# Moving one of twelve float16 residual subtractions of each expert item from VectorE to GpSimd

## What is computed

```python
logits = (h @ w_router + b_router).astype(jnp.float32)
top_val, top_idx = lax.top_k(logits, 4)          # 4 of 32 experts a token
gate = jax.nn.softmax(top_val, axis=-1)
...
gu = xblk @ w_gate_up[e] + b_gate_up[e]
g_lin = jnp.minimum(gu[:, :1024], 7.0)
u_lin = jnp.clip(gu[:, 1024:], -7.0, 7.0)
act = g_lin * jax.nn.sigmoid(1.702 * g_lin) * (u_lin + 1.0)
return act @ w_down[e] + b_down[e]
...
y = y.at[row_tok].add(yb * row_g[:, None])       # rows added back into the stream
```

## Time and profile before

| what | value |
|---|---|
| three timed runs | 2106.95, 2105.22, 2104.69 us; median 2105.22 us |
| the profiled execution's own time | 2105.01 us, its span 2103.2 us |
| TensorE matmul busy | 1981.9 us (94%) |
| VectorE busy | 1527.3 us (73%) |
| ScalarE busy | 1425.2 us (68%) |
| GpSimd busy | 531.3 us (25%) |
| HBM traffic | 234 GB/s over the span; 320 to 340 GB/s in the expert stage |

### The profile page before, as it was taken

How to read it: one execution, slowest core, us unless ns; L and a number is a source line. 1 busy time by engine, 2 the same in 40 slices (tenths; PEclk the granted TensorE clock), 3 DMA queues, 4 the chain that set the end, 5 groups by cost and what they waited for, 6 DMA issues and landing times.

```text
span 2103.2 us, 60172 instructions
## 1 busy us (share of the span) xinstructions
PE 1981.9 (94%) x24649; PEld 1664.8 (79%) x24649; DVE 1527.3 (73%) x2026; ACT 1425.2 (68%) x1810; POOL 531.3 (25%) x413
## 2 busy tenths in 40 slices
PE   6999999999979769999999999999999999999997
PEld 3444874443554469999999999999999999999997
DVE  5331334554472278888998999899899989989995
ACT  4330423666563458777888888788888878888884
POOL 2222211323551232112222321222132122223111
PEclk8999999999999879999999999999999999999999
DMA  5111100000143468999999999999999999999996
GB/s 170 40 41 60 41 21 1 1 1 0 31 138 119 147 208 305 312 330 309 331 323 339 337 324 323 340 328 323 339 335 337 324 334 333 326 337 326 341 321 214
DMA packets 142367, 479.14 MB, mean 228 GB/s; under 512 B 15135, under 2 KB 30239, under 8 KB 142240
## 3 DMA queue, kind: packets, MB, share of 16 engines
q1 hardware_dynamic: 129440, 444.13, 58.8%
q0 software_dynamic: 12864, 34.11, 6.8%
HBM read 457.34 MB, written 34.87 MB: 234 GB/s over the span
## 4 chain that ended last, share of the span: by engine, by line
PE 30%; DVE 15%; issue 12%; ACT 4%; DMA 3%; DVEq 1%; POOL 0%; POOLq 0%; SPq 0%; ACTq 0%
PE banks L1721 28%; DVE region_c L1020 9%; DVE region_b L1557 2%; DMA region_a<-w_down_dram 2%; DVE region_b L1562 1%; ACT region_b L1404 1%; ACT region_b L1408 1%; PE banks L1687 1%; PE banks L1714 1%; ACT region_b L1394 1%; ACT region_b L1392 1%; DVE region_b L1578 1%; DVE region_b L1571 1%; DMA region_b<-rows_out,region_d 1%; DVE region_b L1567 0%
## 5 line engine op out<-in xcount | busy, mean ns | idle before, releaser
L1721 PE MATMUL banks<-region_b,region_c 128*128 128x144 f16 (+1 forms) x18432 | 1198.6, 227 | 32.1 <-DVE region_c L1020 25.3
L1721 PEld LDWEIGHTS banks<-region_b,region_c 128*128 128x128 f16 x18432 | 1181.3, 98 | 39.3 <-DVE region_c L1020 26.6
L1020 DVE TENSOR_TENSOR region_c<-region_a,region_c 128x2048 f16<-128x2048 f32 x256 | 574.4, 2286 | 4.8 <-DMA region_b<-rows_h,region_d 4.3
L1015 ACT ACTIVATE region_c<-region_a 128x2048 f16<-128x2048 f32 x256 | 475.5, 1904 | 22.9 <-PE banks L1721 17.4
L1335 POOL TENSOR_TENSOR region_d<-region_d 80x1 f32<-80x1 f32 x96 | 77.7, 810 | 961.4 <-DVE region_d L1530 643.5
L1020 DVE TENSOR_TENSOR region_c<-region_d,region_c 128x2048 f16<-128x2048 f32 x128 | 287.1, 2284 | 0.0
L1015 ACT ACTIVATE region_c<-region_d 128x2048 f16<-128x2048 f32 x128 | 237.9, 1918 | 0.0
L352 PE MATMUL banks<-region_a,region_d 128*128 128x512 f16 x960 | 209.7, 381 | 1.7 <-PEq L95 1.7
L1417 ACT ACTIVATE region_b<-banks,region_d 80x512 f32<-80x512 f32 x128 | 80.5, 678 | 163.9 <-PE banks L1714 163.9
L352 PEld LDWEIGHTS banks<-region_a,region_d 128*128 128x128 f16 x960 | 94.2, 98 | 117.4 <-issue 6.5
L1324 POOL DMA_INDIRECT region_b<-rows_h,region_d x64 | 136.0, 2125 | 38.0 <-issue 38.0
(11 more groups left out here) (287 smaller groups left out, 2165.7 us busy)
## 6 DMA issues: line engine op xcount, KB each, us to landing
region_d<-w_gate_up_dram SPq DMA_DIRECT2D x128, 1024.0 KB
region_a<-w_gate_up_dram SPq DMA_DIRECT2D x128, 1024.0 KB
region_a<-w_down_dram SPq DMA_DIRECT2D x128, 1024.0 KB
region_d<-w_in_dram SPq DMA_DIRECT2D x14, 1024.0 KB, 5.0
region_b<-x_dram SPq DMA_DIRECT2D x4, 1024.0 KB, 9.5
region_b<-w_out_dram SPq DMA_DIRECT2D x8, 512.0 KB, 3.6
rows_out<-region_b SPq DMA_DIRECT2D x8, 512.0 KB, 2.6
rows_h<-region_b SPq DMA_DIRECT2D x8, 512.0 KB, 2.6
```

The costliest lines, as they stand in the source:

```text
L1015: act.activation(part_hi[r][:, 2 * q:2 * q + 2, :], raw[r][:, 2 * q:2 * q + 2, :], ACT.Copy).then_inc(s_hi9, 1)
L1020: dve.tensor_tensor(part_lo[r][:, at, :], raw[r][:, at, :], part_hi[r][:, at, :], ALU.subtract).then_inc(s_lod, 1)
L1721: mm = pe.matmul(out_ap, a, b, start=(first and s == 0), stop=(k == KT - 1 and s == 2), skip_group_check=True)
```

## The change

The low part of the second half of chunk 4 (`POOL_HALF = (4, 1)`, the second half of the first down chunk) is subtracted by GpSimd, at the end of its item, behind the second scatter-add. VectorE skips it, so `s_lod` counts 11 halves an item and every wait on it is renumbered through `lows`. A new semaphore `s_plo` counts GpSimd's halves; SyncE waits for it before it loads into that half's slot, and TensorE waits for it at the start of down(0).

```diff
-        s_hi9, s_lod = sem("part_hi_ready"), sem("part_lo_ready")
+        s_hi9, s_lod, s_plo = sem("part_hi_ready"), sem("part_lo_ready"), sem("pool_part_lo_ready")
+        POOL_HALF = (4, 1)
+
+        def lows(i, m, q):
+            return i * 11 + (2 * m + q + 1 - ((m, q) >= POOL_HALF))
@@ sync, item_loads
                         for q in range(2):
-                            sp.wait_ge(s_lod, i * (2 * CH) + (2 * m + q + 1))
+                            if (m, q) == POOL_HALF:
+                                sp.wait_ge(s_plo, i + 1)
+                            else:
+                                sp.wait_ge(s_lod, lows(i, m, q))
                             load(sp, e if m < RING else e_next, (m + RING) % CH, q)
@@ gpsimd, item_rows
                     carry_wait(2, i * 3 + (1 if last else 2))
                     scatter(1)
+                    m, q = POOL_HALF
+                    r, at = m % RING, slice(2 * q, 2 * q + 2)
+                    pool.wait_ge(s_hi9, i * (2 * CH) + (2 * m + q + 1))
+                    pool.tensor_tensor(part_lo[r][:, at, :], raw[r][:, at, :], part_hi[r][:, at, :], ALU.subtract).then_inc(s_plo, 1)
@@ vector, low_part
                     for q in range(2):
-                        low_half(dve, c, j, q)
+                        if (j, q) != POOL_HALF:
+                            low_half(dve, c, j, q)
@@ tensor, gate, up and down
-                    pe.wait_ge(s_lod, i * (2 * CH) + (2 * half + 2))
+                    pe.wait_ge(s_lod, lows(i, half, 1))
...
-                    pe.wait_ge(s_lod, i * (2 * CH) + (2 * (2 + half) + 2))
+                    pe.wait_ge(s_lod, lows(i, 2 + half, 1))
...
-                    pe.wait_ge(s_lod, i * (2 * CH) + (2 * (4 + half) + 2))
+                    pe.wait_ge(s_lod, lows(i, 4 + half, 1))
+                    if half == 0:
+                        pe.wait_ge(s_plo, i + 1)
```

## The result

The changed kernel takes 2311.07 us in the median (2308.08 to 2314.2, 4 runs), the kernel before 2104.95 us beside it: 1.0982 times as long, with an interval of 1.0967 to 1.0998, or 206 us slower. The profiled execution took 2310.04 us with a span of 2308.1 us. In the new file line 1024 is VectorE's low part, 1371 GpSimd's, 1733 the expert matmuls, 1342 and 1336 the carry and the scatter-add, 1579, 1583 and 1590 the activation steps.

A forecast was written before the change was run, and what follows sets the result against it. TensorE, with almost no idle time to win, was taken as the bound, down(0) having to wait for GpSimd. 138 us of waits plus 58 us of clock on 2105.0 us gave 2301, said as 2300 us; range 2236 to 2345 us.

The forecast's parts named there:

- A: The forecast itself: down(0) waits for GpSimd and the clock falls in most of these waits; 2300 us, chance 0.77.
- The wait: Ahead of down(0), TensorE waits for GpSimd's half: about 5.4 us a narrow item, 3.85 us a wide one; 138 us net.
- The sum behind the second scatter-add: From the second scatter-add's end to down(0): 0.30 gap, 0.1 VectorE in flight, 4.07 subtraction, 0.1 signal, in us.
- The clock: TensorE's clock falls behind the new wait: 2.0 us a narrow item, about 1.2 us a wide one, 58 us together.
- The first gate half's 2.23 us: Extra time of the stage's first gate half, started at the lower clock: 9.03 us against 6.80 us for the next.
- the 1.8 us: Work lost at half speed after TensorE stood 5.62 us, the clock returning 3.65 us after its restart.
- The 0.88 us ahead of down(1): TensorE's idle stretch before down(1) in each of 26 narrow items goes away by itself, 23 us.
- VectorE beside GpSimd: VectorE loses about 4.07 us in its activation steps while GpSimd subtracts, hidden ahead of down(1) by 0.7 us.
- Loads: SyncE's load into that slot half is issued some 9 us later but still lands in time; costed at nothing.
- Rival B: Down(0) waits for GpSimd but the clock costs nothing or little: 2243 us, chance 0.12.
- Rival C: GpSimd gets its turn late behind busy VectorE, or VectorE's lost time sets down(1): 2372 us, chance 0.07.
- Rival D: At the start of down(0), GpSimd is done before TensorE comes, winning back at most 25.3 us: 2080 us, chance 0.02.

The follow-up runs named there:

- the filling matmuls: The changed kernel with 68 more matmuls of 128 columns, product unread, ahead of TensorE's wait for GpSimd's half: 2251.19 us, 1.0691 against the kernel before.
- the two-pass kernel: The kernel before, with down(1) in two passes, its first 48 matmuls waiting only for the first half of chunk 5: 2087.33 us, 0.9919.
- the one in VectorE's own idle time: The changed kernel with GpSimd given the second half of the next item's gate chunk 1 instead: 2105.83 us, 1.0014 against the kernel before.

## Why the prediction was right, and where its terms were off

The forecast was 2300 us, the median is 2311.07 us, in the range of 2236 to 2345 us, by the mechanism named as A.

- **The wait.** Forecast 138 us net of the 0.88 us stretches; the idle time ahead of the expert matmuls grew by 145.5 us and TensorE's as a whole by 140.3 us, since it idled 5.2 us less elsewhere. The waits themselves are 175.5 us in place of 160 to 170 us: 5.8 us a narrow item against 5.4, and 4.15 us a wide one against 3.85. The sum behind the second scatter-add came out at 4.5 us, as 0.30 + 0.1 + 4.07 + 0.1 had it, but that is luck between its terms: in the item shown GpSimd ended 4.09 us after the scatter-add, without the gap of 0.30 us, and TensorE started 0.44 us after GpSimd, not 0.1 us. GpSimd's own row reads 4.55 us instead of 4.07, because it starts inside the scatter-add's row.
- **The clock.** Forecast 2.0 us a narrow item, 1.2 us a wide one and 58 us in all; measured 8.61 - 6.16 = 2.45 us in the item shown, 57.2/26 = 2.2 us in the mean of the narrow items and 11.2/6 = 1.9 us in that of the wide ones, 64.6 us more busy time in all, and 60 us given back by the filling matmuls. The first gate half's 2.23 us was the nearer row, not the mean of it and the 1.8 us. Both terms were thus some way too small, and the sum with them: 196 us forecast, 205 us measured in the span. The upper bound has a slip as well: 2.8 us for each of 32 items is 90 us, not 87.
- **The 0.88 us ahead of down(1).** It went away in the changed kernel, as said. With the wait ahead of down(1) taken away by TensorE's order alone the kernel gained 16.6 us. Whether that is the most that a relief of VectorE could bring is not shown: in no run did the move to GpSimd relieve VectorE, whose busy time rose each time.
- **VectorE beside GpSimd.** Held for 4 to 5 us in each item, as the two directions of the earlier trace rows had it. VectorE's busy time grew by 87.7 us where 32 x 2.28 = 73 us had been taken off, so 161 us were spent standing, 5.0 us an item. I called it hidden by 0.7 us, and ahead of down(1) it is, by 2.5 us in the item shown (1671.04 to 1673.54), most of it because down(0) ran slower. Ahead of down(0) it is not always: in the six wide items and the last one down(0) starts with an activation step, where I had put it down to GpSimd alone. This is the step that the mechanism had wrong.
- **The clip.** I counted only two-input steps as held. The one-input step with 321 ns is held as well. What that added here wasn't measured: the two-input steps that follow it would most likely have been held anyway.
- **GpSimd's time from elsewhere.** The 4497 ns that the prediction names, and uses for the top of its range only, stands in the Trainium skill ("GPSIMD Engine Reference", section 3.1) for a tensor_tensor add, not for a subtraction.
- **Loads.** Costed at nothing, and right: ScalarE's high parts wait for no load in the changed kernel, while SyncE stands 325.6 us for GpSimd's half in its queue.

Rival B is out: the clock fell, in all items. Rival C is out for this kernel: GpSimd's 32 rows take 4.53 to 4.55 us, so it never stood behind a low part, and VectorE's lost time didn't set down(1). What C describes does occur, though, in the kernel with the subtraction inside the scatter's wait, where GpSimd stood through four VectorE steps. Rival D was the matter of place, and the same kernel shows that with the half ready in time it would still have lost 46 us, not won 25.

What stays open is the rest of the two-pass kernel: whether the new wait ahead of down(0) can be taken away by another order of VectorE's steps wasn't tried.

## What to carry to other kernels

An engine that is 75% idle is no free engine: ask whether it is idle at the place where the result is wanted, and what it shuts out while it works. GpSimd's elementwise step takes about twice VectorE's time and holds VectorE meanwhile, so moving a step across costs VectorE 4 us to save it 2.3 us. Of the three places tried only the one in VectorE's own idle time cost nothing, and none gained. Where the bound engine waits, count its lost clock as a second price; here it was 60 us on top of 140 us.

## What the runs showed of the hardware

- A GpSimd memset, which reads nothing, holds a VectorE tensor_scalar on 320 float32 elements from SBUF to SBUF (longest 4770 ns, median 321 ns) but neither of the two tensor_tensor steps of that size that were running when it began (longest 525 and 544 ns). A GpSimd subtraction holds both (tensor_tensor up to 5472 ns).
- A VectorE copy of 24 elements was held in the same way, for 4.10 us, and one of 8 elements for 4.06 us.
- GpSimd's subtraction stood through four two-input steps of VectorE that ran one behind the other (row of 7.73 us in place of 4.55 us).
- Behind waits of 5.3 to 6.4 us every down(0) of 144 columns was slower (7.5 to 8.6 us in place of 6.16 us). Behind shorter waits of one length the clock fell in some items and not in others: 96 matmuls in 7.80 or 6.16 us behind 1.80 us, 48 matmuls in 4.60 or 3.16 us behind 2.96 us. So one item isn't enough to tell what such a wait costs.
- 68 useless matmuls in each item made a kernel 60 us faster (2311.07 to 2251.19 us).
